# A two-block transformer kernel on one core: two of eight channel tiles of a depthwise convolution on GpSimd, channel sums on VectorE, and moved steps around them

## The reference, cut to what matters

```
z = h @ w_in                                   # 256 x 4800, cut into the parts below
ua, ub, q_lat, kv_lat, k_r, gate_logits = ...
u = ua * sigmoid(ub)                           # 256 x 1024
u = causal_depthwise_conv(u, conv_w, conv_b)   # 31 taps per channel
u = silu(layer_norm(u, conv_norm_g, conv_norm_b))   # mean and variance over the 1024 channels
y_a = u @ w_conv_out
q  = rms_norm(q_lat, q_norm_g) @ w_uq          # 384 wide latents
kv = rms_norm(kv_lat, kv_norm_g) @ w_ukv       # 256 wide latents
o = attention(rope(q), rope(kv), 8 heads, causal)
y_b = o @ w_attn_out
return (sigmoid(g_a) * y_a + sigmoid(g_b) * y_b) @ w_out
```

## Time and profile before

| | us |
|---|---|
| median of 3 runs | 1164.62 |
| lowest, highest | 1163.64, 1167.79 |
| the profiled execution's own time | 1170.42 |
| its span, first to last instruction | 1168.3 |
| PE busy | 1120.9 (96%) |
| DVE busy | 819.2 (70%) |
| ACT busy | 564.9 (48%) |
| POOL busy | 42.0 (4%) |

### The profile page before, as it was taken

One profiled execution on the slowest core, in us unless ns is written; L12 is line 12 of the kernel. 1 busy time (PEld: TensorE's weight loads), 2 busy tenths in 40 slices (PEclk: granted clock), 3 DMA queues, 4 the chain that ended last, 5 costly groups with the idle time before them and its releaser, 6 DMA issues.

```text
span 1168.3 us, 20613 instructions
## 1 busy us (share of the span) xinstructions
PE 1120.9 (96%) x8460; PEld 950.5 (81%) x8460; DVE 819.2 (70%) x1162; ACT 564.9 (48%) x712; POOL 42.0 (4%) x48
## 2 busy tenths in 40 slices
PE   8899999999999896899999999999999999999998
PEld 7788888889788686787888887788878888999996
DVE  4665544558398465979999987899997777555554
ACT  4545643354564445364433464354465655444443
POOL 0000000000001310101111000000000000000000
PEclk9999999999999999999999998999999999999999
DMA  9585456643233111659999954354441354564632
GB/s 320 166 273 185 157 177 207 215 167 123 88 128 114 40 22 40 210 189 344 355 339 358 313 178 131 106 187 152 147 144 36 112 184 142 176 211 149 212 111 107
DMA packets 129220, 204.89 MB, mean 175 GB/s; under 512 B 11177, under 2 KB 86718, under 8 KB 129151
## 3 DMA queue, kind: packets, MB, share of 16 engines
q1 hardware_dynamic: 121716, 176.58, 45.8%
q0 software_dynamic: 6560, 25.19, 6.3%
q10 hardware_dynamic: 874, 2.12, 0.5%
HBM read 201.78 MB, written 1.05 MB: 174 GB/s over the span
## 4 chain that ended last, share of the span: by engine, by line
PE 76%; DVE 13%; ACT 5%; DMA 4%; issue 2%; SPq 0%; DVEq 0%; POOL 0%; ACTq 0%
PE ps L685 21%; PE ps L687 20%; PE ps L686 20%; DVE wl L2445 4%; PE ps L1109 2%; DVE wide L3130 2%; DMA raw<-in_ab_w_in 2%; DMA raw<-in_ffn_w_up 2%; PE ps L895 1%; PE ps L762 1%; ACT wh L1704 1%; PE ps L1022 1%; PE ps L1580 1%; PE ps L1141 1%; PE ps L1414 1%
## 5 line engine op out<-in xcount | busy, mean ns | idle before, releaser
L2445 DVE TENSOR_TENSOR wl<-raw,wh 128x2048 fp32r<-128x2048 f32 (+2 forms) x155 | 347.5, 2248 | 131.9 <-ACT wh L1704 131.8
L685 PE MATMUL ps<-wh,xh 128*128 128x512 f32 (+4 forms) x1112 | 412.1, 371 | 14.0 <-DVE wl L2445 9.0
L687 PE MATMUL ps<-wl,xh 128*128 128x512 f32 (+4 forms) x1112 | 403.2, 363 | 0.0
L686 PE MATMUL ps<-wh,xl 128*128 128x512 f32 (+4 forms) x1112 | 403.0, 362 | 0.0
L1704 ACT ACTIVATE wh<-raw 128x2048 fp32r<-128x2048 f32 (+2 forms) x155 | 288.7, 1881 | 95.4 <-PE ps L687 70.0
L685 PEld LDWEIGHTS ps<-wh,xh 128*128 128x128 f32 x1112 | 211.0, 190 | 51.5 <-DVE wl L2445 9.5
L687 PEld LDWEIGHTS ps<-wl,xh 128*128 128x128 f32 x1112 | 210.8, 190 | 32.4
L686 PEld LDWEIGHTS ps<-wh,xl 128*128 128x128 f32 x1112 | 211.2, 190 | 31.3 <-issue 1.0
L685 PE MATMUL ps<-wh,gh 128*128 128x512 f32 x280 | 109.7, 392 | 0.8 <-DVE wl L2445 0.8
L686 PE MATMUL ps<-wh,gl 128*128 128x512 f32 x280 | 109.2, 390 | 0.0
L687 PE MATMUL ps<-wl,gh 128*128 128x512 f32 x280 | 109.1, 390 | 0.0
(11 more groups left out here) (388 smaller groups left out, 1194.0 us busy)
## 6 DMA issues: line engine op xcount, KB each, us to landing
wide<-in_w_ada POOLq DMA_DIRECT2D x24, 1024.0 KB, 10.1
raw<-in_ffn_w_gate SPq DMA_DIRECT2D x44, 512.0 KB, 4.4
raw<-in_ffn_w_up SPq DMA_DIRECT2D x44, 512.0 KB, 5.5
raw<-in_ffn_w_down SPq DMA_DIRECT2D x22, 1024.0 KB, 5.2
raw<-in_w_mlp_in SPq DMA_DIRECT2D x16, 1024.0 KB, 7.1
raw<-in_w_mlp_out SPq DMA_DIRECT2D x16, 1024.0 KB, 5.2
raw<-in_w_in SPq DMA_DIRECT2D x16, 512.0 KB, 4.8
raw<-in_w_in SPq DMA_DIRECT2D x8, 1024.0 KB, 5.0
```

Of the source, the lines that this page charges most:

```text
L685: pe.matmul(o, lh, rh, start=start, stop=False)
L686: pe.matmul(o, ll, rh, start=False, stop=False)
L687: return pe.matmul(o, lh, rl, start=False, stop=stop)
L2445: v.tensor_tensor(wl[:, s, 0:width], raw[:, s, 0:width], f32(wh[:, s, 0:width]), ALU.subtract).then_inc(lo_ready[s], 1)
```

## The change

Five things change, in one step.

1. Tiles 2 and 3 of the convolution go from VectorE to GpSimd: 31 multiplications and 31 additions of 128x512 (both tiles at once), each waiting for the one before by a semaphore. They begin when the second `u_put` is done. VectorE's list loses 62 steps. The calls `conv(n)` still add up to 217, so the list runs out early: 151 steps stand ahead of attention, 4 more directly ahead of it as part of a call for 16, none in it.
2. Sums over channels: VectorE first adds the eight tiles into one (`tile_sum`, three additions of 128x1024, 128x512, 128x256), and TensorE then needs one matmul in place of eight, for the mean and for the variance.
3. The latents get a home of their own (`latent`), so that they are made after the third gate block and not after the last. The wait and the dummy matmuls ahead of `uq` go.
4. The split of `("glu", 1, 1)` moves ahead of the first `glu` result, and the angles move behind it.
5. Calls of `conv`, splits and gating are moved a little, and two dummy activations load a table of ScalarE's early.

```
+            term, total = W3(1, 2, 1536, 512), W3(2, KT)[:, 2:4, :]
+            pool.wait_ge(S("u_put"), B("u_put") + 2)
+            for k in range(CK):
+                src = U_PAD(wide)[:, 2:4, k:k + SEQ]
+                nc.gpsimd.tensor_tensor(term, src, pair(CONVW, CK, k), ALU.mult).then_inc(S("conv_pool"), 1)
+                pool.wait_ge(S("conv_pool"), B("conv_pool") + 2 * k + 1)
+                old = total if k else pair(ROWS["conv_b_2"], 1, 0)
+                nc.gpsimd.tensor_tensor(total, term, old, ALU.add).then_inc(S("conv_pool"), 1)
+                pool.wait_ge(S("conv_pool"), B("conv_pool") + 2 * k + 2)
...
-CONV_DVE = ((0, 1), (2, 3), (4, 5, 6))
+CONV_DVE = ((0, 1), (4, 5, 6))
...
-            pe.wait_ge(S("gatev"), B("gatev") + 8)
-            spin(0, 12)
-            pe.wait_ge(S("lq.xl"), B("lq.xl") + 5)
+            pe.wait_ge(S("gatev"), B("gatev") + 6)
+            pe.wait_ge(S("lq.xl"), B("lq.xl") + 3)
...
-                for n, (kt, steps) in enumerate(order):
...
-                    m = pe.matmul(ps[:, 4, 0:SEQ], ones[:, :], cv[:, kt, :], start=n == 0, stop=n == KT - 1)
-                m.then_inc(S("cmean"), 1)
+                pe.wait_ge(S("cv_sum"), B("cv_sum") + 1)
+                pe.matmul(ps[:, 4, 0:SEQ], ones[:, :], sq[:, 0, :], start=True, stop=True).then_inc(S("cmean"), 1)
...
             split(("glu", 1, 0))
-            act.wait_ge(S("angle"), B("angle") + 1)
-            act.activation(lowr[:, 0:64], lowr[:, 0:64], ACT.Sin)
-            act.activation(lowr[:, 64:128], lowr[:, 64:128], ACT.Sin).then_inc(S("sincos"), 1)
+            act.activation(unused, eps, ACT.Sigmoid)
+            split(("glu", 1, 1))
...
-                else:
+                if c == 2:
                     for kt in range(5):
                         act.wait_ge(S("lq.T"), B("lq.T") + kt // 2 + 1)
-                        act.activation(xh[:, kt, :], ps[:, 4 + kt // 2, (kt % 2) * SEQ:(kt % 2 + 1) * SEQ], ACT.Identity,
+                        act.activation(latent(0, kt), ps[:, 4 + kt // 2, (kt % 2) * SEQ:(kt % 2 + 1) * SEQ], ACT.Identity,
...
+            def tile_sum(first):
+                for n in (4, 2, 1):
+                    src = cv if n == 4 and first else sq
+                    m = v.tensor_tensor(sq[:, 0:n, :], src[:, 0:n, :], src[:, n:2 * n, :], ALU.add)
+                    if n > 1:
+                        link(m)
+                m.then_inc(S("cv_sum"), 1)
+            v.wait_ge(S("conv_step"), B("conv_step") + 5 * CK)
+            v.wait_ge(S("conv_pool"), B("conv_pool") + 2 * CK)
+            v.wait_ge(S("conv_pe"), B("conv_pe") + CONV_PE)
+            v.wait_ge(S("at.o"), B("at.o") + NH)
+            tile_sum(True)
             split(("attn_out", 1, 0))
...
+            v.wait_ge(S("csq"), B("csq") + 2)
+            tile_sum(False)
...
+            attention_gated(0)
             v.wait_ge(S("cvar"), B("cvar") + 1)
```

More of the change, by code:

```diff
@@ L1646, in _ @@
                     pe.wait_ge(S("at.xl"), B("at.xl") + NH)
[L1647 to L1650, removed]
+                half(s, range(4, 8), o, 512, False, True).then_inc(w_used[s], 1)
             ym = W3(9, NT)
@@ L2236, in _ @@
             u_put(3)
-            split(("lat", 1, 1), ("gate", 0, 0))
+            split(("gate", 0, 0), ("gate", 0, 1))
             used(act, ("lat", 1, 1))
@@ L2240, in _ @@
                 act.activation(lat[:, t, QL:704], ps[:, 2 + t, 0:KL + ROPE], ACT.Copy).then_inc(S("lat"), 1)
-            split(("gate", 0, 1))
             split(("gate", 1, 0))
@@ L2359, in _ @@
             act.activation(lowr[:, 256:512], lowr[:, 256:512], ACT.Sqrt).then_inc(S("cv_std"), 1)
+            act.activation(unused, eps, ACT.Silu)
+            split(("conv_out", 0, 1))
             for k in range(2):
@@ L3148, in _ @@
                      .then_inc(S("glu"), 1)
-                for n, name in enumerate(nxt[2 * c:2 * c + 2]):
+                if c:
+                    conv(3)
+                else:
+                    angles()
+                for n, name in enumerate(nxt[max(2 * c - 1, 0):2 * c + 1]):
                     split(name)
@@ L3153, in _ @@
                     if c:
-                        conv(7)
+                        conv(5 if c == 3 else 6 + n)
                 if c == 0:
                     conv(10)
-            for name in [("lat", 1, 1), ("gate", 0, 0), ("gate", 0, 1)]:
-                split(name)
-                conv(7)
+            split(("lat", 1, 1))
+            conv(5)
+            split(("gate", 0, 0))
+            conv(5)
+            split(("gate", 0, 1))
             lat = W(3, 0, 2 * 704).rearrange("p (t n) -> p t n", t=NT)
@@ L3270, in _ @@
                 v.tensor_tensor(cv[:, o, :], cv[:, o, :], cmean.unsqueeze(1).to_broadcast([P, 4, SEQ]), ALU.subtract).then_inc(S("cv_c"), 1)
[L3271 to L3278 removed]
+            split(("attn_out", 1, 1))
+            v.wait_ge(S("csq"), B("csq") + 2)
+            tile_sum(False)
             gates = wide[:, 6 * 2048:8 * 2048].rearrange("p (t n) -> p t n", t=NT)
@@ L3289, in _ @@
             attention_gated(0)
+            v.wait_ge(S("cvar"), B("cvar") + 1)
+            v.tensor_scalar(lowr[:, 256:512], ps[:, 5, 0:SEQ], 1.0 / D, EPS, ALU.mult, ALU.add).then_inc(S("cv_ss"), 1)
+            v.wait_ge(S("cv_std"), B("cv_std") + 1)
+            link(v.reciprocal(lowr[:, 768:1024], lowr[:, 256:512]))
+            for k in range(2):
+                o = slice(4 * k, 4 * k + 4)
+                v.tensor_tensor(cv[:, o, :], cv[:, o, :], lowr[:, 768:1024].unsqueeze(1).to_broadcast([P, 4, SEQ]), ALU.mult).then_inc(S("cv_n"), 1)
+            split(("conv_out", 0, 0))
             for k in range(2):
```

122 lines of the change are left out of this document (64 added, 58 removed).

## The result

| | us |
|---|---|
| kernel before, median of 4 (lowest, highest) | 1164.33 (1163.64, 1167.79) |
| changed kernel, median of 4 (lowest, highest) | 1201.72 (1199.74, 1203.97) |
| ratio, 95% interval | 1.0316 [1.0285, 1.0346] |
| profiled execution of the changed kernel, its span | 1199.74, 1197.9 |
| forecast | 1199 |

What follows compares the result with a forecast made beforehand. TensorE and VectorE were both taken as full from 736 to 858 us. VectorE's loss of 60 less 6.4 and 7.1 gives +46.5, less 12.0 from the moves +34.5, on 1164.6: 1199 us, range 1177 to 1214 (8 in 10: 1142 to 1212).

Steps and rivals of the forecast that it cites:

- The loss: VectorE beside GpSimd's 62 convolution operations: taking turns at SBUF costs VectorE 60 us.
- The full end: Upper bound of VectorE's loss: nothing lies beside GpSimd's operations, each waited for whole, 69 us.
- The moved steps: All terms besides GpSimd's two tiles together: 18.5 us less if VectorE is not slowed.
- `glu`: Turn into `("glu", 1, 1)`: TensorE's wait of 2.9 and slow clock of 3.1 us go, 6.0 us less.
- Latents: Ahead of `uq`: TensorE's idle time and dummy matmuls go, 4.1 us less.
- Sums: Channel sums ahead of `conv_out`: one matmul each in place of eight, 5 us less.
- The rest: Wait ahead of `("ukv", 0)` 1.4, TensorE's other idle time 1, attention without VectorE's steps 1 us less.
- The sum: Whole kernel: VectorE's +46.5 us less 12.0 gives +34.5, so 1199 us.
- Rival 1: VectorE and GpSimd do not hinder each other: -18.5, 1146 us (1138 to 1156); chance 0.29.
- Rival 2: VectorE goes first, GpSimd runs in its gaps, first channel sum waits 40 us: +21, 1186 us; chance 0.07.
- Rival 3: The engines exclude each other in part, a third to half of 60: +5 to +12, about 1173; chance 0.08.
- Rival 4: Moves bring less than half, nothing is hindered: -3 to -8, about 1159 us; chance 0.06.

Runs made afterwards that it cites:

- late sixteen-tap kernel: Changed kernel with GpSimd doing 16 of 31 taps, begun when the rotary products are done, 15 taps of two tiles left out: 1153.87 us (one run).
- second profiles: Repeat profiles of the unchanged kernel before (stage 211.4 us) and of the changed kernel without GpSimd's tiles, angles first as before (stage 202.0 us).
- second profile of before: The kernel before, unchanged, profiled a second time: 1166.49 us (one run), stage 211.4 us.
- kernel with fills: Changed kernel with GpSimd's 62 operations replaced by 124 memsets of 128x512 that read nothing, tiles 2 and 3 left out: 1148.59 us (one run).
- moves-only run: Changed kernel with tiles 2 and 3 given back to VectorE, nothing on GpSimd, the other changes kept: 1151.78 us, 0.9875 of the kernel before.

## Why the prediction was right, step by step

**The mechanism held.** The engines take turns where VectorE reads a second input from SBUF and GpSimd reads too, and such an instruction is free where GpSimd only writes, or where one of its inputs is in PSUM. The Trainium skill (SBUF — State Buffer, Who interferes with whom) says just this of instructions with two SBUF inputs, the free write and the free PSUM input among it, and the traces agree: 1352 ns a step beside reads, 477 beside fills, 0.74 us for two products from PSUM. That engines meet only through semaphores, as said ahead of the prediction, holds for their order alone: here they also met at SBUF.

**The loss, forecast 60 us, was 54.5.** The full end (69), which goes with the Trainium skill's wait for the whole instruction (the same section), doesn't agree with the traces, and the measurement decides. Outside the splits an operation of GpSimd took 1.31 us from start to start, and each of the 62 cost VectorE 0.88. The 0.15 us of a step that I let lie beside GpSimd was too little. How the rest overlaps isn't shown. With its wait on its own semaphore, bounded by 0 and 0.2 us, GpSimd took 1.18 and 1.43 from start to start against 1.00 and 1.23 in the earlier trace rows. The difference is near the upper end, but not all of it is the wait: with VectorE idle at the end of the late sixteen-tap kernel it was 1.12 in place of 1.18.

**GpSimd's end was forecast near 848 and came at 827.7.** My figure put all of VectorE's work between GpSimd's operations. In the trace a whole step fits into GpSimd's own pitch, and it is splits that hold GpSimd (2.4 to 3.2 us for one operation). So VectorE's time for a step tripled (0.40 to 1.3 us from start to start) and GpSimd's time for an operation hardly changed.

**TensorE's idle time**, forecast some 45 us between 736 and 850, is 38.7 in that window, 30.7 of them on "DVE wl". The difference is of the size of the shorter loss.

**The moved steps, forecast -18.5, measured -14.4 to -17.2** by the stage (211.4 or 214.2 less 197.0) and -14.6 by the ratio. Term by term:
- `glu`, forecast 6.0: 3.4 or 5.0. The 2.9 of the wait is right and always there. The 3.1 for the clock was taken from one execution and is there in some only; with the clock at 1.00 the move is worth 3.4, with half the fall 5.0.
- Latents, forecast 4.1: 1.9. The step that failed is the size. TensorE got all 4.1, but the text itself named what is late next as "due about 2 us before", and still counted the whole 4.1. These 2 us were all there was to gain.
- Sums, forecast 5: 6.0.
- The rest, forecast 3.4, is what is left: 1.5 to 5.9 us by the profiles that are paired, not tried singly. The pair that lost alike to the clock at the `glu` turn (the second profiles, 1.7 us each) gives 14.4 - 5.0 - 1.9 - 6.0 = 1.5. The wait ahead of `("ukv", 0)` is gone from TensorE's list of waits.

**The sum.** Forecast +34.5; the stage says +32.7 against the first profile of before and +35.5 against the second, and the medians +37.4. My base of 1164.6 came with a profiled execution that lay 5.8 above it. The second profile of before (1166.49) took 3.9 back: 2.8 in the stage, where the clock rose sooner behind one wait and didn't fall behind another, and 1.3 in the stretch ahead.

**Where the sum was lucky.** That the total fits so well is in part luck, since its errors cancel. Up to the queries' rotation the forecast had 60 - 6.4 - 7.1 - 6.0 = +40.5 us. There VectorE begins the rotation 179.4 us into the stage against 136.8 in the first profile of before and 135.6 in the second: +42.5 or +43.8. So the loss was 5.5 smaller than forecast, and what was set against it (19.5: steps gone, idle time that absorbs, the `glu` turn) came to only 12.0 or 10.7. The idle time is where it shows: of the 7.1, the held stretch had 0.9 to absorb with. Behind the rotation the forecast had -6, and the stage says -9.8 or -8.3.

**The rivals.** Rival 1 (no hindrance) fell: beside reads the step went to 1352 ns. The kernel with fills comes to its 1146: 1148.59 where before took 1166.95, a ratio of 0.984 (one run), which is 1146 from 1164.33. The single terms fit less well than their sum. Rival 2 (VectorE first) fell: GpSimd's own stretch, from 733.24 to 827.73, was 94.5 us for 62 operations, 1.52 each with the holds by splits against 1.31 without, while VectorE's steps came at a third of their pace. Rival 3 (partial) fell by size, since VectorE lost 54.5 us and not 20 to 30. Its numbers were also not worked out rightly: by the forecast's own sum (the loss less 13.5 and 12.0) a third to a half of the 60 gives -5.5 to +4.5, and +5 to +12 belongs to a loss of 30.5 to 37.5. Rival 4 (moves bring little) fell with the moves-only run.

**The best version** is the one with the moves only: 0.9875 of the time before, some 52 us below the changed kernel.

## What to carry to other kernels

Before work goes from VectorE to GpSimd, list what VectorE reads meanwhile, and its TENSOR_SCALARs with one SBUF input too. Beside steps and splits with two SBUF inputs, each GpSimd operation cost VectorE two thirds of its own length, so that 62 operations took 54.5 us to save 62 steps of 0.40; in attention, where VectorE reads mostly PSUM, 32 of them cost 0.8 to 3.2 in all. And where two engines are full side by side, a wait taken from one is worth only the slack of the other (here 1.9 of 4.1 us). A gain that comes from the clock is taken from more than one profile: here the same wait cost 0 to 3 us of it.

## What the runs showed of the hardware

- A VectorE TENSOR_SCALAR with a single SBUF input is held too: 1.28 us for 256 elements beside GpSimd's reads (L3137 above) and 0.6 to 0.7 beside its fills, against 0.41 and 0.35 in the kernel with the moves only. It is the kind of instruction that the earlier trace rows shows at double pace.
- GpSimd's fills of 128x512, 530 ns each, hindered no instruction with two SBUF inputs.
- A GpSimd two-input operation of 512 elements that waits for its predecessor's semaphore took 0.12 to 0.2 us more from start to start (1.12 with VectorE idle and 1.18 beside it, against 1.00; 1.43 against 1.23).
- Behind a TensorE wait of 2.8 to 3.0 us the granted clock fell to 0.50 in some executions of a kernel and stayed at 1.00 in another, worth 0 to 3 us. Behind a wait of 1.4 us it did the same (0.62 as the mean of 4 us, or 1.00), worth 1.5 us.
